# Chunk stage of a hybrid retention and RWKV-7 layer: seeds, refinement rounds and the bonus product stand at other places in the order

## What is computed

```python
def _rwkv7_scan(s0, w, k, v, kk, a, r=None):
    def step(s, xt):
        wt, kt, vt, kkt, at = xt[:5]
        sa = jnp.einsum('bhvk,bhk->bhv', s, -kkt)
        s = (s * wt[:, :, None, :] + sa[..., None] * (kkt * at)[:, :, None, :]
             + vt[..., None] * kt[:, :, None, :])
        return s, jnp.einsum('bhvk,bhk->bhv', s, xt[5])
...
    bonus = jnp.sum(qu['r'][None] * st['k'] * r_k, axis=-1, keepdims=True).sum(0) * st['v']
```

## Time and profile before

| | us |
|---|---|
| median of 3 runs | 4214.6 (4200.79 to 4215.76) |
| the profiled execution, its own time | 4209.31 |
| its span in the trace | 4207.5 |
| PE busy in the span | 3800.6 (90%) |
| DVE, ACT, POOL busy | 2296.5 (55%), 1933.0 (46%), 520.3 (12%) |
| chunk stage, first to last of the 36 seed products on PE | 990.07 |

### The profile page before, as it was taken

One profiled execution on the slowest core, in us unless ns is written; L12 is line 12 of the kernel. 1 busy time (PEld: TensorE's weight loads), 2 busy tenths in 40 slices (PEclk: granted clock), 3 DMA queues, 4 the chain that ended last, 5 costly groups with the idle time before them and its releaser, 6 DMA issues. The chain is left out here.

```text
span 4207.5 us, 93593 instructions
## 1 busy us (share of the span) xinstructions
PE 3800.6 (90%) x39634; PEld 3197.0 (76%) x39634; DVE 2296.5 (55%) x3808; ACT 1933.0 (46%) x2958; POOL 520.3 (12%) x563
## 2 busy tenths in 40 slices
PE   7999999999978898998896869899499999999993
PEld 6778878888868888888885757677388888888882
DVE  5533524434347777777775955454554444445445
ACT  5533434434346666666662343333144444444443
POOL 1000000000011221221220313300000000000000
PEclk9999999999989999999997979999599999999996
DMA  7566665555532222222223356553456666656567
GB/s 247 194 185 187 180 191 156 155 153 160 148 117 77 67 71 78 64 74 78 60 62 110 106 181 212 200 182 132 171 210 210 212 210 220 216 210 210 210 216 283
DMA packets 333046, 673.68 MB, mean 160 GB/s; under 512 B 37436, under 2 KB 218276, under 8 KB 314120
## 3 DMA queue, kind: packets, MB, share of 16 engines
q1 hardware_dynamic: 310568, 581.99, 42.2%
q0 software_dynamic: 22112, 86.41, 7.0%
HBM read 525.16 MB, written 143.15 MB: 159 GB/s over the span
## 5 line engine op out<-in xcount | busy, mean ns | idle before, releaser
L112 PE MATMUL fro__acc<-fro__hT_hi,fro__wh 128*128 128x512 f32 (+1 forms) x1608 | 626.1, 389 | 7.5 <-DVE fro__hT_lo L2531 4.6
L113 PE MATMUL fro__acc<-fro__hT_hi,fro__wl 128*128 128x512 f32 (+1 forms) x1608 | 614.0, 382 | 0.0
L114 PE MATMUL fro__acc<-fro__hT_lo,fro__wh 128*128 128x512 f32 (+1 forms) x1608 | 613.7, 382 | 0.0
L2015 DVE TENSOR_TENSOR pre__wl<-fin__raw,pre__wh 128x4096 fp32r<-128x4096 f32 x96 | 424.7, 4424 | 318.0 <-ACT pre__wh L1965 318.0
L2537 DVE TENSOR_TENSOR fro__wl<-prj__w,fro__wh 128x1024 fp32r<-128x1024 f32 x201 | 246.1, 1225 | 640.5 <-ACT fro__wh L2341 640.5
L1965 ACT ACTIVATE pre__wh<-fin__raw 128x4096 fp32r<-128x4096 f32 x96 | 348.6, 3631 | 192.4 <-PE exp__acc L114 192.3
L112 PE MATMUL exp__acc<-pre__wh,exp__xh 128*128 128x512 f32 x1024 | 401.9, 393 | 0.7 <-DVE exp__xl L2020 0.7
L114 PE MATMUL exp__acc<-pre__wl,exp__xh 128*128 128x512 f32 x1024 | 399.5, 390 | 0.0
L113 PE MATMUL exp__acc<-pre__wh,exp__xl 128*128 128x512 f32 x1024 | 399.3, 390 | 0.0
L112 PEld LDWEIGHTS fro__acc<-fro__hT_hi,fro__wh 128*128 128x128 f32 x1608 | 304.6, 189 | 73.8 <-issue 18.3
L113 PEld LDWEIGHTS fro__acc<-fro__hT_hi,fro__wl 128*128 128x128 f32 x1608 | 304.7, 189 | 59.1 <-issue 3.6
(11 more groups left out here) (433 smaller groups left out, 8031.9 us busy)
## 6 DMA issues: line engine op xcount, KB each, us to landing
fin__raw<-in_w_x SPq DMA_DIRECT2D x96, 2048.0 KB, 7.5
prj__w<-in_w_z SPq DMA_DIRECT2D x201, 512.0 KB, 4.1
s_zT<-fro__zo SPq DMA_DIRECT2D x128, 256.0 KB, 4.6
fro__wm<-in_w_mod POOLq DMA_DIRECT2D x16, 1024.0 KB, 5.7
mix__gate<-s_zT SPq DMA_DIRECT2D x64, 256.0 KB, 3.6
prj__xin<-in_tokens SPq DMA_DIRECT2D x18, 512.0 KB, 5.3
rwc__kS<-s_kS SPq DMA_DIRECT2D x36, 256.0 KB, 3.2
rwc__kkn<-s_kkn SPq DMA_DIRECT2D x36, 256.0 KB, 3.4
```

The lines of the kernel that those rows point to most:

```text
L112: pe.matmul(out, sh, mh, start=first, stop=False)
L113: pe.matmul(out, sl, mh, start=False, stop=False)
L114: return pe.matmul(out, sh, ml, start=False, stop=last)
L2015: ve.tensor_tensor(wl[s][:, :, :], raw[s][:, :, :], wh[s][:, :, :], ALU.subtract).then_inc(w_lo, 1)
```

## The change

Only the order of steps in the chunk stage changes, with one bank and the waits that belong to it. No instruction is added or removed, and the work for each slab is the same.

- PE: `inverse_seed(n)` and the last `learning(h + 2)` stand at the end of the iteration behind both `errors`, which now follow each other behind all three `turn`s. The seeds had stood at the start of the next iteration, behind `bonus`.
- Rounds 0, 1 and 2 of `refine` for slab `p` stand between `couple` and `double` of levels 0, 1 and 2. Before, round 0 was in the iteration before, behind its `errors`, and rounds 1 and 2 at levels 0 and 1.
- The chain of `h - 2`, chunk 1, and of `p`, chunk 0, stands about one level later: `values` and `from_state` of `h - 2` behind `double(0)`, `solve` behind `double(1)`, `state` behind `double(2)`; those of `p` behind `couple(3)` and `couple(4)`; `state(p, 0)` between the two halves of `pairs`, `outputs(h - 2, 1)` between `double(3)` and `couple(4)`, `outputs(p, 0)` behind `decays`.
- `bonus(n)` stands behind `couple(4)`, and writes bank `PB1` where it had written `XB0`. `decays` now waits for ACT's copy of it, and `bonus` for `learning`'s sigmoid and for the copy of the outputs of slab `j - 3`.
- ACT and DVE follow: `copies(0, n)` stand at the end of the iteration, `outputs` of chunk 1 before `copies(4)`, `outputs` of chunk 0 behind the three `turned`, `running(n)` behind the refinement of round 0.

The diff, cut to its core:

```diff
@@ scalar: bonus, and the loop over h
-                cp(bo[:, :], XB[0][:, 0:C], "bonc")
+                cp(bo[:, :], PB[1][:, 0:C], "bonc")
...
                 if exists(h - 1):
                     right_side(h - 1, 0)
...
                 if exists(h - 2):
                     outputs(h - 2, 1)
+                if inverting:
+                    copies(4, h)
+                if prepare:
+                    bonus(n)
                 if exists(h - 1):
                     solved(h - 1, 0)
...
                     for k in range(3):
                         turned(n, k)
+                if exists(h - 1):
+                    outputs(h - 1, 0)
+                if prepare:
+                    copies(0, n)
@@ vector: the loop over h
                     levels(0, h)
                 if exists(h - 1):
-                    refine(1, h - 1, 0)
-                    refine(1, h - 1, 1)
+                    refine(0, h - 1, 0)
+                    refine(0, h - 1, 1)
                 if prepare:
+                    running(n)
                     centred(n)
...
-                    refine(0, h, 0)
-                    refine(0, h, 1)
-                if h + 2 < SLABS:
-                    running(h + 2)
@@ tensor: decays and bonus
                 if j:
-                    pe.wait_ge(S["asg"], at("asg", j - 1))
-                if j >= 4:
-                    pe.wait_ge(S["yc1"], at("yc1", j - 4))
+                    pe.wait_ge(S["bonc"], at("bonc", j - 1))
...
             def bonus(j):
-                pe.wait_ge(S["trc"], at("trc", j, 2))
+                pe.wait_ge(S["asg"], at("asg", j))
+                if j >= 3:
+                    pe.wait_ge(S["yc1"], at("yc1", j - 3))
                 pe.wait_ge(S["bonp"], at("bonp", j))
                 for q in range(4):
-                    m = mm(XB[0][32 * q:32 * q + 32, 0:C], ones32[:, :], bon[:, q, :], start=True, stop=True, skip_group_check=True)
+                    m = mm(PB[1][32 * q:32 * q + 32, 0:C], ones32[:, :], bon[:, q, :], start=True, stop=True, skip_group_check=True)
```

More of the change, by code:

```diff
@@ L531, in _ @@
                 turned(0, k)
+            bonus(0)
+            copies(0, 0)
             decays(1)
             learning(1)
-            bonus(0)
             for h in range(SLABS + 2):
@@ L949, in _ @@
                 if inverting:
-                    inverse_seed(h)
+                    couple(0, h)
+                if exists(p):
+                    refine(0, p, 0)
+                    refine(0, p, 1)
+                if inverting:
+                    double(0, h)
                 if exists(h - 2):
@@ L954, in _ @@
                 if inverting:
-                    couple(0, h)
+                    couple(1, h)
                 if exists(p):
@@ L981, in _ @@
                 if inverting:
-                    couple(3, h)
+                    couple(4, h)
+                if prepare:
+                    bonus(n)
                 if exists(p):
                     solve(p, 0)
-                if inverting:
-                    double(3, h)
-                    couple(4, h)
-                if exists(p):
-                    state(p, 0)
-                if h + 2 < SLABS:
-                    decays(h + 2)
                 if inverting:
@@ L996, in _ @@
                 if exists(p):
+                    state(p, 0)
+                if prepare:
+                    pairs(n, 1)
+                if h + 2 < SLABS:
+                    decays(h + 2)
+                if exists(p):
                     outputs(p, 0)
                 if prepare:
-                    pairs(n, 1)
-                    turn(n, 0)
+                    for k in range(3):
+                        turn(n, k)
                 if inverting:
                     errors(h, 0)
+                    errors(h, 1)
                 if prepare:
-                    turn(n, 1)
-                    turn(n, 2)
-                if inverting:
-                    errors(h, 1)
-                    refine(0, h, 0)
+                    inverse_seed(n)
                 if h + 2 < SLABS:
                     learning(h + 2)
-                if inverting:
-                    refine(0, h, 1)
-                if prepare:
-                    bonus(n)
 def rwkv_mix(nc, T):
```

49 lines of the change are left out of this document (20 added, 29 removed).

## The result

| | before | after |
|---|---|---|
| median of 8 runs, us | 4218.14 | 4241.45 |
| ratio to before, 95% interval | | 1.0057 (1.0037 to 1.0077) |
| profiled execution, us | 4209.31 | 4228.04 |
| chunk stage, first to last seeds on PE | 990.07 | 1013.04 |
| from the last seeds to the end of the span | 1992.4 | 1994.0 |

The change made the kernel slower by 0.6%, about 24 us: a small loss, but clear of the interval. 4166 us and a gain had been forecast. One of the eight runs of after, 4368.96 us at a lower granted clock, is a slow one and counts for nothing in the ratio. The whole difference lies in the stage that the change touches: 23.0 us more there, within 6 us of the same on either side of it.

A forecast was written before the change was run, and what follows sets the result against it. PE was taken as the bound, with idle waits and clock drops. From the profiled 4209.3 us, 48.7 go (21 idle pieces, 27 clock), giving 4160.6; with 5.3 added for the median, 4166 us, range 4144 to 4211.

The forecast's parts named there:

- What bounds the kernel: Chunk stage: PE is the bound, 24.9 us of matmuls plus 2.62 idle a slab; low clock costs 27.3 us in all.
- End of the iteration: PE's wait for ErH before round 0 goes, 1.57 us a slab, since seeds, learning and couple(0) stand between.
- Levels 0 and 3, state of chunk 1: PE idle before double(0) 0.1 us, at level 3 0.2, before state of chunk 1 0.1 instead of 0.61.
- Level 4: New PE wait: couple(4) behind outputs and ACT's yo copy, 1.1 us idle instead of 0.20, bounds 0.9 and 1.4.
- End, the new wait: PE's second errors waits for ACT's yo0 behind the turned copies: 0.5 us idle, bounds 0.2 and 1.2.
- The instructions are the same, so the 24.9 us of matmuls stay.: PE in each slab: matmul time stays 24.9 us; with 2.0 idle the slab takes 26.9 us at 2.4 GHz.
- all these cost nothing: Bonus product, its new waits, decays' wait, slab loads and store on SP, and POOL's order add no time.
- The clock: Chunk stage: longest idle piece falls from 1.57 to about 1.1 us, so the drops go, gaining 27.3 us.
- the slower one: Rival: a clock drop in each slab behind couple(4)'s or errors' wait, 2.3 us each, 4246 us; chance 0.08.
- two signs of being wrong: Forecast is wrong if the two new waits together exceed 2.2 us, or the stage's mean clock still shows 0.96.
- the second rival: New waits eat the old one: slab stays at 27.5 us, only the clock gains, 4187 us; chance 0.12.
- the first rival: The clock keeps dropping as now: only the 21 us of idle pieces are gained, 4194 us; chance 0.15.

The follow-up runs named there:

- s_before: The kernel before with the six large loads of each slab from the third on cut to two columns; ratio to before 0.9879.
- e5: The kernel before with only the six slab loads issued some 20 us later, behind the last copy of the inverse; ratio to before 0.9892.
- e6: The kernel before with only seeds and learning put ahead of round 0, level 0 copies following on ACT; ratio to before 0.9888.
- s_after: The changed kernel with the six large loads of each slab from the third on cut to two columns; ratio to before 0.9912.
- e4: The changed kernel with ACT's copy yo0 ahead of the second coupling and turned copies, and the slab loads issued later; ratio to before 0.987.
- e10: The changed kernel with yo1 behind level 4's copies, yo0 early, bonus behind solve of chunk 0, and loads issued later; ratio to before 0.9876.
- e11: e10 with DVE's level 4 mask ahead of scaled, and state of chunk 0 ahead of both halves of pairs; 4140.38 us, ratio to before 0.9813.
- e7: The changed kernel with only the six slab loads issued later, behind the last copy of the inverse; ratio to before 0.9927.
- e8: e6 with the six slab loads issued later; 4140.95 us, ratio to before 0.9815.

## Why the prediction was wrong, step by step

*What bounds the kernel.* Right: PE, in latency, with the idle pieces as read. Wrong in one reading: the drops do not all stand behind the long wait. By their rows ten of before's thirteen stand there, three do not, and s_before and e5 keep every one of these 35 waits and have two drops and one. One of the two periods that it shows already stands elsewhere: the one from 2205.49 is 9.6 us before the last seeds. That the long piece causes the drops was argued from where they stood; the runs show that it takes the loads at their old place beside it. The price of the clock was too low as well: the mean of 28.29 us has the three incomplete slabs in it, and by slabs 2 to 33 the low clock cost 32.9 us, not 27.3.

*End of the iteration.* Right: the 1.57 us go. In e6, with this alone, some 0.8 us come back at the seeds, on `v_t`; in after the wait of `errors` stands ahead of them and covers it.

*Levels 0 and 3, state of chunk 1.* Right within the bounds. Before `double(0)` stands about 0.1 us, `couple(3)` has no wait of its own, and `state` of chunk 1 waits 3 us in all 35 slabs, where it had 14.7. ACT's table load takes its 1.28 us as in the earlier trace rows and the exponential starts 0.01 us behind it:

```profile
2042.40 1.28 ACT L440 ACT_TABLE_LOAD   x1
2043.69 0.63 ACT L440 ACTIVATE rwc__e_bk<-rwc__D 128x512 f32<-128x512 f32 x1
```

The drain of some 1380 ns that the Trainium skill (ScalarE: Activation LUTs, What ACT_TABLE_LOAD costs) gives beside the load isn't to be seen here either; the trace does not agree, and the row was the right one to go by.

*Level 4.* Right in place and cause, 0.95 against 1.1. *End, the new wait.* Right in place and cause, 0.94 on average (31.8 / 34) against 0.5. The step took PE's cover as 7.2 us from the lengths of the rows; the difference of two sums of 7 to 8 us is not known to 0.3, and for the 0.2 us that it took off for the modelled ends it had no row. Without the loads (s_after) the idle pieces make 2.27 us in a slab at full clock, where 2.0 had been forecast, and 2.64 in the old order (s_before).

*"The instructions are the same, so the 24.9 us of matmuls stay."* This step failed, twice, and with it the slab of 26.9 us: it measured 28.11. First, 0.34 of the 1.21 us that it was off: without any collision the slab takes 27.25 us in the old order and 27.26 in the new (27.24 in both with the loads late), although 0.37 us less of it is idle: the rest of the slab grew by as much. Between the starts of matmuls, in the clean slabs of s_before and s_after, the places that lost their wait give back 2.9 us (1.78 behind the last product of `errors`, 0.72 behind the doublings, 0.40 behind `solve`), the two with a new one take 2.25 (1.23 behind `outputs`, 1.02 between the halves of `errors`), and 0.65 is spread over the steps, most of it in `outputs` (0.33), in the couplings (0.17) and in the seeds' products (0.16). So the hole at `couple(4)` takes 1.2 us or more from start to start, where 0.95 is called idle. I take the modelled ends for the reason, which count the latency of the last product as busy; that is argued, not shown. An idle piece is then no full price of a hole. Second, 0.87 us of the 1.21: the 24.9 us contained stalls, 15.2 / 35 = 0.4 us a slab, whose size depends on what PE does while the loads run. They became 1.0 us, and with the loads late the slab at full clock falls by 0.87, from 28.11 to 27.24, where before's falls by 0.24. The loads cost before 40.8 us of its stage and after 50.8, from the runs without them, and the prediction had written of them "all these cost nothing". They are issued at the last transpose; in the old order they ran from about 1 us before the seeds to 5 behind them, in the new from 1 to 7 behind, and the stalls stand at 5.4 to 12.3.

*The clock.* This step failed too: drops "go", and there are 21. Of the 71.6 us by which the stage missed its forecast, 35 x 26.9 = 941.5, the clock accounts for 36.5 and the slab at full clock for 38.7, (28.11 - 26.9) x 32; the three incomplete slabs give back 3.6. So the two failed steps cost about the same. Against the kernel before, though, the clock is only 3.6 us worse: the forecast missed by it because it had booked before's whole loss as a gain. Of the rivals, the slower one named the mechanism, more drops, at the places where they now stand: behind the wait of `couple(4)` and behind stalls. It asked for 21 drops and got 21, but its number, 4246 us, is met by the 4241 measured only by luck: by its own sum 21 drops would have made no change, and a drop cost 36.5 / 21 = 1.7 us, not 2.3; the rest of the loss is the slab at full clock, which it took as improved. It had 0.08, because the new pieces are shorter than the old. That reason was no reason: in e4, 27 drops stand behind a piece of 0.9 to 1.1 us and in e10, 31 beside one of 1.3 to 1.7, while 35 pieces of 1.6 us in e5 bring one. Of the prediction's own two signs of being wrong, the two new waits together stayed under 2.2 us (1.9), and the stage's clock of 0.95 showed it.

The chances have a slip in their sum: the forecast, the second rival and half of the first make 0.745, not 0.72.

The Trainium skill (TensorE: Matmul & The Clock Gate, A second HAM failure mode) describes a kernel in which short idle pieces between groups of matmuls, repeated in each round, make the clock go to and fro. It stood in the prediction beside the first rival and was discounted by a row (0.61 us had never done it). e10 and e11 agree with it: one piece of 1.3 to 1.7 us a slab, 31 drops; the piece mostly removed, 4 drops. e5 doesn't fit it as it is told, and no run tells what the difference is.

*What stays open.* By what the chip decides on a drop: the length of one idle piece alone doesn't do it. The second rival of the experiments, that the slabs' length matters, was not excluded: in e10 the drops have settled 27.31 us apart, exactly once a slab. And why a packet of PE's instructions starts later beside the loads: that it does, and that PE's stalls end when it has come, is in the traces; where it is held up is not.

## What to carry to other kernels

Matmuls "that stay the same" have a cost only together with what runs beside them: before a reordering is priced, look for pieces of idle time that no engine ends inside a step, and for the transfers and the packets of instructions that run at that moment; here the loads belonged beside the part with few, long instructions. Count each removed wait against the next slack on every engine, ACT's queue of copies first: here one copy behind three others cost 45 us, and every hole closed opened the next (`couple(4)`, `bonus`, `double(4)`). Compare like slabs: one short slab at the start of a stage can turn a mean of few. And where the clock drops, try the parts of a change alone: the seeds moved and the loads issued later make 1.85%, while the full change made a loss.

## What the runs showed of the hardware that was not expected

- PE stalls of 0.3 to 2.2 us inside a step of equal matmuls, each ending 1.1 to 1.6 us behind the end of a 16 KB packet on the queue q8 and, in 41 of 41 cases of after, a multiple of 256 of PE's instructions from the others, to within one. They come while or just behind a burst of loads that has the DMA engines at some 0.9, where PE starts some 31 matmuls a microsecond beside it, and hardly where it starts 15: 15.2 us in 22 stalls before, 34.7 in 41 after, 0.0 to 1.1 us in e4, e5, e7, e8 and e10, which move the same bytes later, and 3.4 in e11.
- A granted clock that is low for longer in a faster kernel: at 26.17 us a slab (e10) for 102.4 us in 31 drops, at 27.24 (e5) for 3.4 in one. A drop of 3.4 us costs 1.2 us there; before's, mostly of 6.8 us, cost 3.0 each (32.9 us in 11).
- A wait of 1.6 us in each slab that leaves the clock alone (e5: one drop), beside waits of 0.9 to 1.1 us (e4) and of 1.3 to 1.7 (e10) that don't.
